# Decoder step: the sample stage begun in the last attention step's tail, w_out split early, and the spare rows' copies spread over attention steps

## What is computed

```python
q_g, k_g, v_g, r_g, log_a, q_a, k_a, v_a, gate_a, gate_b = combined_projection(h, w_in, gk_up, gk_bias)
# prompt: chunked gated linear attention and sliding-window attention
# sample: one recurrent step on a stored state, and attention over 128 cached keys
o_g, s_new = gla_run(q_g, k_g, v_g, log_a, gla_s0, ...)
o_a, k_new, v_new = swa_sample(q_a, k_a, v_a, win_k, win_v, rel_bias, sinks)
merged = sigmoid(gate_a) * gla_output(o_g, r_g) + sigmoid(gate_b) * o_a
h1 = layer_norm(ALPHA * h + merged @ w_out, ln1_g, ln1_b)
f  = hier_moe(h1, ...)          # 32 experts, each token goes to 2
h2 = layer_norm(ALPHA * h1 + f, ln2_g, ln2_b)
```

## Time and profile before

| | |
|---|---|
| median of 3 runs | 1911.17 us (1908.79 to 1911.86) |
| profiled execution, own time | 1909.03 us |
| its span, first to last instruction | 1906.9 us |
| busy: PE, PEld, DVE, ACT, POOL | 91%, 77%, 64%, 46%, 16% |
| mean granted TensorE clock | 0.944 of full speed |
| first step of stage B to end of the last | 331 to 965 us |
| sample stage | 965 to 1052 us |
| output stage | 1052 to about 1205 us |

### The profile page before, as it was taken

The page is one execution under the profiler, slowest core; times in us unless marked ns, Lnnn a source line. Parts: engine busy times, 40 slices in busy tenths (PEclk is TensorE's granted clock), DMA queues, the critical chain, the costliest instruction groups (busy, mean ns, idle before and its releaser), DMA issues. The chain is left out here.

```text
span 1906.9 us, 28797 instructions
## 1 busy us (share of the span) xinstructions
PE 1734.5 (91%) x9022; PEld 1463.8 (77%) x9022; DVE 1221.0 (64%) x1695; ACT 883.9 (46%) x1446; POOL 306.3 (16%) x386
## 2 busy tenths in 40 slices
PE   4899999899899999999978899379999999999955
PEld 4889999688788878878846788268888888888832
DVE  6411110577778767777753333868988988988917
ACT  4322221344344434444411122338778778788723
POOL 3200000122412232232210111010000010010025
PEclk9889999899999999999967899579999999999978
DMA  6379521434333333422359424379999999999854
GB/s 207 108 238 289 171 68 52 142 103 144 115 123 125 126 130 103 158 90 89 95 191 321 146 99 185 123 273 397 419 411 414 417 411 409 419 413 408 330 214 194
DMA packets 183312, 422.90 MB, mean 222 GB/s; under 512 B 24976, under 2 KB 123168, under 8 KB 158424
## 3 DMA queue, kind: packets, MB, share of 16 engines
q1 hardware_dynamic: 129776, 321.93, 45.8%
q0 software_dynamic: 20048, 69.06, 10.2%
q10 hardware_dynamic: 33408, 30.94, 4.6%
HBM read 354.83 MB, written 78.55 MB: 227 GB/s over the span
## 5 line engine op out<-in xcount | busy, mean ns | idle before, releaser
L1801 DVE TENSOR_TENSOR wm_lo<-raw,wm_hi 128x2048 fp32r<-128x2048 f32 x192 | 434.3, 2290 | 70.1 <-ACT wm_hi L1297 66.5
L1297 ACT CAST wm_hi<-raw 128x2048 fp32r<-128x2048 f32 x192 | 363.4, 1912 | 72.9 <-PE PS L1934 44.8
L1932 PE MATMUL PS<-w_hi,hT_hl 128*128 128x512 f32 (+1 forms) x584 | 232.9, 399 | 12.0 <-DMA hT_hl<-hl_dram 7.1
L1933 PE MATMUL PS<-w_lo,hT_hl 128*128 128x512 f32 (+1 forms) x584 | 227.0, 389 | 0.0
L1934 PE MATMUL PS<-w_hi,hT_hl 128*128 128x512 f32 (+1 forms) x584 | 226.6, 388 | 0.0
L1932 PE MATMUL PS<-wm_hi,xT_hi 128*128 128x512 f32 x512 | 203.7, 398 | 2.9 <-DVE xT_lo L1863 2.9
L1934 PE MATMUL PS<-wm_hi,xT_lo 128*128 128x512 f32 x512 | 200.8, 392 | 0.0
L1933 PE MATMUL PS<-wm_lo,xT_hi 128*128 128x512 f32 x512 | 200.3, 391 | 0.0
L1972 PE MATMUL PS<-xa_hi,wn 128*128 128x384 f32 x480 | 162.1, 338 | 0.2 <-ACT ev L1063 0.2
L1974 PE MATMUL PS<-xa_hi,wn 128*128 128x384 f32 x480 | 161.3, 336 | 0.0
L1973 PE MATMUL PS<-xa_lo,wn 128*128 128x384 f32 x480 | 161.2, 336 | 0.0
(11 more groups left out here) (340 smaller groups left out, 3403.2 us busy)
## 6 DMA issues: line engine op xcount, KB each, us to landing
raw<-in_w_gate SPq DMA_DIRECT2D x64, 1024.0 KB, 6.7
raw<-in_w_up SPq DMA_DIRECT2D x64, 1024.0 KB, 7.5
raw<-in_w_down SPq DMA_DIRECT2D x64, 1024.0 KB, 8.4
hT_hl<-hl_dram POOLq DMA_DIRECT2D x70, 512.0 KB, 5.2
braw<-in_w_in SPq DMA_DIRECT2D x16, 1024.0 KB, 6.2
obuf_dram<-yb ACTq DMA_DIRECT2D x32, 512.0 KB, 8.2
nd_dram<-ev ACTq DMA_DIRECT2D x72, 192.0 KB, 2.1
nd<-nd_dram SPq DMA_DIRECT2D x36, 384.0 KB, 3.4
```

The lines of the kernel that those rows point to most:

```text
L1297: act.copy(wm_hi[:, j], raw[:, j]).then_inc(m_hi[j // 4], 1)
L1801: dve.tensor_tensor(wm_lo[:, j], raw[:, j], BF(wm_hi[:, j]), ALU.subtract).then_inc(m_lo[j // 4], 1)
L1932: pe.matmul(out, x_hi, w_hi_, start=start, stop=False)
L1933: pe.matmul(out, x_hi, w_lo_, start=False, stop=False)
```

## The change

Three edits, which share the queues:

1. The sample stage starts without the common wait. PE, VectorE and GpSimd each wait only for what they touch; SP loads `gath` and `aqo` right after the last gates product. `S_MERGED` no longer holds back the output stage: `o_transposes(0, 0)` is put between the sample scores and the softmax on PE, `o_low(0, 0)` between the copy of `oT` and the merge on VectorE, ScalarE waits for `S_PV`, and L2150 writes to PSUM banks 6 and 7 so that banks 0 and 1 are free. The first two loads of `hh` come before the state stores.
2. Two of the four pieces of `w_out` are loaded and split in the last group's steps, where earlier groups split the next group's weights; the other two are loaded at its end and split in ScalarE's and VectorE's waits of the sample stage.
3. The two 4608 KB copies of the spare rows become 18 copies of 512 KB, two each in blocks 3, 4 and 5 of groups 0 to 2, issued by SP between `ka_load` and the next `nd_load`.

The diff, cut to its core (text in brackets stands for code that only moves or stays):

```diff
--- wait values
-    S_..., S_OTC, S_MERGED = (..., 21, 22)
+    S_..., S_OTC, S_OTREAD, S_MERGED = (..., 21, 22, 23)
...
--- SP (the sync engine's queue), attention steps
+        def spare_rows(k):
+            for a in range(2):
+                sp.dma_start(obuf_dram[(NE + a * NB + k) * P:(NE + a * NB + k + 1) * P, :], h_dram[k]).then_inc(s_out, 16)
...
                 ka_load(g, b, s, n0 + b)
+                if g < 3 and b in (3, 4, 5):
+                    spare_rows(3 * g + b - 3)
                 if g + 1 < G and b in (1, 7):
                     wide_load(g + 1, 0 if b == 1 else 2)
                 if g + 1 < G and b in (2, 8):
                     wide_load(g + 1, 1 if b == 2 else 3)
+                if g + 1 == G and b in (2, 3):
+                    wout_load(b - 2)
...
+        wout_load(3)
         sp.wait_ge(b_gg, upto(G * NB - 1))
+        stash_done(sp, G - 1)
+        (gath and aqo loads, moved up from behind stageB_done)
         state_load(0)
         state_load(1)
+        wout_load(2)
         stageB_done(sp)
-        (gath and aqo loads)
         state_load(2)
         state_load(3)
-        wout_load(0)
-        wout_load(1)
...
-        wout_load(2)
-        wout_load(3)
...
-        for a in range(2):
-            sp.dma_start(obuf_dram[(NE + a * NB) * P:(NE + (a + 1) * NB) * P, :],
-                         h_dram.rearrange("b p n -> (b p) n")).then_inc(s_out, 16)
         for k in range(2):
             mg_load(k, k)
+        sp.wait_ge(s_pe, S_SC)
+        h_load(0, 0)
+        h_load(1, 1)
         sp.wait_ge(s_dve, S_STATE[G - 1] + 1)
         (four stores of gla_state_sample, then the S_MERGED wait, as before)
-        h_load(0, 0)
-        h_load(1, 1)
         mg_load(2, 0)
-        sp.wait_ge(s_out, 16 * (G + 2))
+        sp.wait_ge(s_out, 16 * (G + 2 * NB))
--- GpSimd
-        stageB_done(pool)
+        pool.wait_ge(b_gg, upto(G * NB - 1))
--- ScalarE
+        def out_high(c):
+            act.wait_ge(w_raw[4 + c % 2], 16 * (c // 2 + 1))
+            act.wait_ge(b_gg, upto((G - 1) * NB - 1))
+            act.copy(wo_hi[:, 2 * c:2 * c + 2].rearrange("p k n -> p (k n)"), raw[:, 4 + c % 2]).then_inc(b_hi, 1)
...
                 for j in pieces:
-                    if j < 2:
+                    if j < 2 and g + 1 < G:
                         wide(g + 1, j)
+                    elif j < 2:
+                        out_high(j)
...
         stageB_done(act)
-        for c in range(4): (wait for the load and copy to wo_hi)
+        out_high(2)
+        out_high(3)
...
-        act.wait_ge(s_dve, S_MERGED)
+        act.wait_ge(s_pe, S_PV)
         (o_high(0, 0), o_high(1, 1), ... as before)
--- VectorE
+        def out_low(c):
+            dve.wait_ge(b_hi, upto(G * WIDE + c))
+            dve.tensor_tensor(wo_lo[:, 2 * c:2 * c + 2] ..., raw[:, 4 + c % 2], wo_hi[:, 2 * c:2 * c + 2] ..., ALU.subtract).then_inc(b_lo, 1)
...
                 for j in pieces:
-                    wide(g + 1, j)
+                    if g + 1 < G:
+                        wide(g + 1, j)
+                    elif j:
+                        out_low(2 - j)
...
-        stageB_done(dve)
+        dve.wait_ge(b_gg, upto(G * NB - 1))
+        stash_done(dve, G - 1)
         (in the loop over g of the state updates:)
-            dve.wait_ge(b_hi, upto(G * WIDE + g))
-            dve.tensor_tensor(wo_lo[:, 2 * g:2 * g + 2] ...).then_inc(b_lo, 1)
         mark(dve.reduce_sum(s8[:, 0], oQ, X), s_dve)
+        stageB_done(dve)
+        out_low(3)
+        out_low(2)
         dve.wait_ge(s_pe, S_SC)
...
         mark(last, s_dve)                 (oT copied)
+        o_low(0, 0)
         dve.wait_ge(act_s, 12)
...
-        link(dve.tensor_tensor(oQ, PS[0:NS, 0:2] ..., gath[:, :, 2], ALU.mult))
+        mark(dve.tensor_tensor(oQ, PS[0:NS, 6:8] ..., gath[:, :, 2], ALU.mult), s_dve)
+        dve.wait_ge(s_dve, S_OTREAD)
         mark(dve.tensor_tensor(oS, oS, oQ, ALU.add), s_dve)
-        dve.wait_ge(s_dve, S_MERGED)
         dve.wait_ge(o_small, 96)
-        o_low(0, 0)
         o_low(1, 1)
--- TensorE
-        stageB_done(pe)
-        pe.wait_ge(b_ko, upto(G - 1))
+        pe.wait_ge(b_stg, G)
+        for done in (b_bs, b_pc, b_pd, b_vrc, b_va, b_eg):
+            pe.wait_ge(done, upto(G * NB - 1))
...
         pe.wait_ge(s_win, 16 * 9)
+        pe.wait_ge(b_ko, upto(G - 1))
+        pe.wait_ge(b_oa, upto(G * NB - 1))
...
         last.then_inc(s_pe, 1)            (scores done)
+        pe.wait_ge(s_dve, S_SSQ - 1)
+        o_transposes(0, 0)
         pe.wait_ge(s_dve, S_ST)
...
-                last = pe.transpose(PS[0:NS, g // 2, c:c + HD], oT[:, h, g, :], ident[0:HD, 0:HD])
+                last = pe.transpose(PS[0:NS, 6 + g // 2, c:c + HD], oT[:, h, g, :], ident[0:HD, 0:HD])
...
-        pe.wait_ge(b_lo, upto(G * WIDE - 1 + 4))
-        pe.wait_ge(s_dve, S_MERGED)
-        pe.wait_ge(o_small, 96)
...
         def o_logits(b):
+            pe.wait_ge(s_dve, S_OTREAD)
+            pe.wait_ge(o_small, 96)
...
-        o_transposes(0, 0)
         o_transposes(1, 1)
+        pe.wait_ge(b_lo, upto(G * WIDE - 1 + 4))
         o_product(0, 0)
```

More of the change, by code:

```diff
@@ L670, in ka_load, with wout_load @@
                 sp.dma_start(ka[s][half * HD:(half + 1) * HD, :], nd_dram[g, b, 0:HD, 4 * P:5 * P]).then_inc(b_kd, 16)
+        wout = A["w_out"][0].rearrange("(k p) n -> p k n", p=P)
+        def wout_load(c):
+            if c >= 2:
+                sp.wait_ge(b_lo, upto(G * WIDE + 3 - c))
+            sp.dma_start(raw[:, 4 + c % 2].rearrange("p (k n) -> p k n", k=2),
+                         wout[:, 2 * c:2 * c + 2, :]).then_inc(w_raw[4 + c % 2], 16)
         sp.wait_ge(n_acc, len(units))
@@ L774, in h_load @@
             sp.dma_start(hh[s][:], h_dram[ds(blk(b), 1)].rearrange("o p n -> p (o n)")).then_inc(e_x[s], 16)
+        sp.wait_ge(s_pe, S_SC)
+        h_load(0, 0)
+        h_load(1, 1)
+        sp.wait_ge(s_dve, S_STATE[G - 1] + 1)
+        for g in range(G):
+            sp.dma_start(R["gla_state_sample"][0, :, g].rearrange("n k e -> k n e"), st[:, g]).then_inc(s_out, 16)
+        sp.wait_ge(s_dve, S_MERGED)
+        sp.dma_start(mg_dram[0, 0:NS, :], oS.rearrange("n g e -> n (g e)")).then_inc(s_new, 16)
+        sp.wait_ge(s_new, 48)
         def h1_store(b, s):
@@ L1185, in step @@
                 act.copy(va[s][:], PS[:, 5, 0:HD]).then_inc(b_va, 1)
-                if 2 in pieces:
+                if 2 in pieces and g + 1 < G:
                     wide(g + 1, 2)
@@ L1220, in _ @@
                 step(n0 + 2 + 2 * i, s0_, (n0 + 3) // 2 + i, False)
-            step(n0 + 5, s1_, (n0 + 6) // 2, False, (0,) if more else ())
-            step(n0 + 6, s0_, (n0 + 7) // 2, False, (1,) if more else ())
+            step(n0 + 5, s1_, (n0 + 6) // 2, False, (0,))
+            step(n0 + 6, s0_, (n0 + 7) // 2, False, (1,))
             step(n0 + 7, s1_, (n0 + 8) // 2, False)
-            step(n0 + 8, s0_, (n0 + 9) // 2, False, (2,) if more else ())
+            step(n0 + 8, s0_, (n0 + 9) // 2, False, (2,))
         stageB_done(act)
-        for c in range(4):
-            act.wait_ge(w_raw[4 + c % 2], 16 * (c // 2 + 1))
-            act.copy(wo_hi[:, 2 * c:2 * c + 2].rearrange("p k n -> p (k n)"), raw[:, 4 + c % 2]).then_inc(b_hi, 1)
+        out_high(2)
+        out_high(3)
         for a in range(8):
@@ L1607, in _ @@
                 step(n0 + 2 + 2 * i, s0_, (n0 + 3) // 2 + i, False, 0)
-            step(n0 + 5, s1_, (n0 + 6) // 2, False, 0, (0,) if more else ())
-            step(n0 + 6, s0_, (n0 + 7) // 2, False, 0, (1,) if more else ())
+            step(n0 + 5, s1_, (n0 + 6) // 2, False, 0, (0,))
+            step(n0 + 6, s0_, (n0 + 7) // 2, False, 0, (1,))
             step(n0 + 7, s1_, (n0 + 8) // 2, False, 0)
-            step(n0 + 8, s0_, (n0 + 9) // 2, False, 0, (2,) if more else ())
+            step(n0 + 8, s0_, (n0 + 9) // 2, False, 0, (2,))
             if g:
@@ L1685, in _, with o_low @@
         mark(last, s_dve)
+        def o_low(b, s):
+            dve.wait_ge(t_hi, upto(NB + b))
+            dve.tensor_tensor(mT_lo[s][:], PS[:, 0:2].rearrange("p a n -> p (a n)"), BF(mT_hi[s][:]), ALU.subtract).then_inc(t_lo, 1)
+        o_low(0, 0)
         dve.wait_ge(act_s, 12)
@@ L2134, in _, with o_transposes @@
         last.then_inc(s_pe, 1)
+        def o_transposes(b, s):
+            pe.wait_ge(h_in[s], 16 * (use(b, s) + 1))
+            pe.wait_ge(t_lo, upto(b - 1))
+            transposes(0, mg[s], KC).then_inc(t_T, 1)
+        pe.wait_ge(s_dve, S_SSQ - 1)
+        o_transposes(0, 0)
         pe.wait_ge(s_dve, S_ST)
```

35 lines of the change are left out of this document (10 added, 25 removed).

## The result

| | before | after |
|---|---|---|
| median of 7 runs each (lowest to highest), us | 1911.17 (1908.79 to 1914.93) | 1922.96 (1919.53 to 1930.26) |
| span of the profiled execution, us | 1906.9 | 1921.2 |
| mean granted clock | 0.944 | 0.944 |

The ratio is 1.0068, with a 95% interval of 1.0050 to 1.0085: the changed kernel is 0.7% slower, about 12 us. The forecast was 1906.0, a gain, and the time lies above the range.

The account below looks back on a forecast made before the run. It took PE, with small products and long pauses between stage B and the output stage, as the bound. Gains 2.2 - 1.6 + 7.5 - 0.7 = 7.4, less 2.7 and 0.6, left 4.1 us; forecast 1906.0, range 1900.5 to 1914.5.

Parts of the forecast that it names:

- 2.2: Start of the sample stage: gain in us up to `outer(1)`, limited by the state load rather than `outer(0)`'s 3.4.
- 1.6: Middle of the sample stage: us lost by putting `o_transposes(0, 0)` between the scores and the first softmax transpose.
- 7.5: End of the sample stage: us gained as value product to first output product shrinks from 11.94 to 4.4.
- the clock's 0.7: Output stage's first product: us lost to a longer low clock after thin work, bounds 0 and 1.8.
- What the spare rows' leaving gives back: nothing: Sample stage: 0 us gained by removing the spare copies, since nothing on the chain waits for a DMA after 984.75.
- 0.3 a step, the least of the waits seen: Stage B, blocks 3 to 5 of three groups: spare copies cost 2.7 us over nine steps, between 0 and 17.
- rival C: Stage B, blocks 4 to 6: copies hold up `hT` in all nine steps, deciding from 0.76 us each; 1914, chance 0.18.
- far case: Stage B: whole 2.8 us burst ahead of `hT`, 0.8 in hand; 2.0 us lost a step, nine 18, kernel 1920.
- signs of being wrong: Stage B waits above 0.8 us, waiting for `mg_load(2, 0)`, state loads no earlier, or over 4 us low clock in first product.
- `w_out` at 0.6: Stage B, last group: `w_out` loads in block 3 and at block 8's end cost 0.3 us each, range 0 to 3.9.
- B: Rival: stage B feels nothing from the new transfers and the 7.4 us gain is kept; 1903, chance 0.20.
- D: Rival: the sample stage gives only 0.8 us, state loads no earlier and clock rising late; 1909.5, chance 0.20.

Follow-up runs that it names:

- e8: The kernel before with only the spare rows' copies moved into stage B, issued behind the landing of the `hT` load: 1911.15 us, ratio 1.0001.
- e5: The kernel before with only the sample stage's early start; spare rows and all four `w_out` pieces stay in the sample stage: 1913.65 us, ratio 1.0016.
- e1: The kernel before with only the spare rows' 18 copies moved into the attention steps, as in the changed kernel: 1926.33 us, ratio 1.0076.
- e4: The changed kernel with each spare copy cut into rows of 4 KB instead of 32 KB, same bytes and place: 1925.44 us, ratio 1.0061 against before.
- e7: The changed kernel with one 512 KB copy a step ahead of `hT`, the other half one copy in the sample stage: 1906.12 us, ratio 0.9983 against before.
- e3: The changed kernel with the same 18 copies issued only after the next `hT` load has landed: 1905.74 us, ratio 0.9958 against before.
- e2: The changed kernel with the spare rows back in the sample stage as two large copies: 1910.02 us, ratio 0.9972 against before.
- e10: The kernel before with only the head groups' weight loads (`wide_load`) moved behind the `hT` load's landing: 1907.14 us, ratio 0.9975.
- e6: The changed kernel with spare copies, `wide_load`s and three `w_out` loads of stage B behind the `hT` load's landing: 1899.7 us, ratio 0.9949 against before.
- e11: The kernel before with the sample stage's early start, spare copies and `wide_load`s behind `hT`'s landing, `w_out` in the sample stage: 1898.0 us, ratio 0.9922.
- e9: The kernel before with the sample stage's early start and spare copies behind `hT`'s landing, `w_out` loaded and split as before: 1905.77 us, ratio 0.9977.

## Why the prediction was wrong

**Edit 1 was right, part by part.** With both traces laid on stage B's last scores, `outer(0)` starts at 976.9 in before's time (977.1 was said) and `outer(1)` at 985.3 (985.5), where PE started it at 987.5: 2.2 us for the **2.2**. `o_transposes(0, 0)` lies between scores and softmax, 1.90 long; from the scores' end to the value product's start it is 5.7 us instead of 4.4, 1.3 for the **1.6**. The last stretch is 4.39 for 4.4, the **7.5**. Only the clock's 0.7 did not come: full clock was there 1.3 us after the first product's start, before's 1.7. S gave 8.4 for 7.4. The `mg_load(2, 0)` with its 3 us to spare made no wait.

**"What the spare rows' leaving gives back: nothing" held for the kernel before (e8), not for the changed one.** The argument was that nothing on before's chain waits for a DMA after 984.75. But edit 1 itself pulls the first reader of `mg` 15 us forward, and e5 shows 8.5 us of wait there if `w_out` and spare rows are still ahead of it. That the 0 held in the sum was luck: edits 2 and 3 were in and had cleared the queue. The step counted a thing on the old chain that should have been counted on the new one.

**The term that failed is "0.3 a step, the least of the waits seen", nine steps, 2.7.** It measured 14.1, 1.6 a step (14.7 in e1, 15.8 in e4). The mechanism was in the prediction: rival C has the copies holding up `hT`, the decision point of 0.76 us, and a far case of 2.0 a step and 1920. Its place was one block late. Rival C and the signs of being wrong name blocks 4, 5 and 6; the copies hold up the `hT` of the block that issues them, 3 to 5, and the waits stood in blocks 3 and 5 and not in 4 or 6. The runs came close to the far case, by two amounts that no term had:

- The wait itself was 8.6 us over six steps, 1.4 in each of the six. The prediction had all that is needed: 2.8 us of copies, 0.8 us in hand, a `wide_load` of the same size that cost up to 1.93. Passing time less what is in hand gives 2.0 a step, an upper figure for the 1.4. The reason to choose the least was that contiguous pieces pass more quickly than pieces of 1 KB. e4 refutes it for 4 against 32 KB: what counts is how many bytes are ahead (e7: half of them, hardly a wait), and whether they are ahead at all (e3: behind, no wait). Three steps in nine were spared, because the stall before them turned the order round; no one counted on that.
- The low clock behind a stall was counted in the sample stage alone. In stage B it came behind three of the six waits, about 5.1 us for 8.6 of waiting; e1 has the same (8.9 and three dips), e4 8.7 and four.

**`w_out` at 0.6 was 2.5**, the same mistake on two loads. The other **5.0** of stage B have no term either; they lie in steps that waited as before but had more of the low clock. No run ties them to the copies: the same steps cost 0.7 more than before in e1, 1.8 in e4, which has all three edits, and 1.5 less in e3. How much of them is this one execution stays open.

**Rivals.** B fell (e1). D fell: the stretch gave its gain. C was right in mechanism, one block off in place, with 14 against its 10.4 and 18; its chance of 0.18 was too low, since before's own rows showed the wait behind five of six loads of this size, and three such steps in a row in each group.

Shown by runs: that edit 3 makes the loss (e1, e2), that it is the order of copies and `hT` (e3), by their bytes (e4, e7), and that before paid the same behind its own loads (e10, e6). The split of the 14.1 into waits and clock is read from traces, and three of them agree (after, e1, e4). Open: the 5.0, and what sets the clock in the sample stage.

## What to carry to other kernels

A bulk transfer without a deadline should be issued behind the load that the bound engine needs next, by a wait on that load's landing; the same 18 copies cost some 14 us ahead of it and nothing behind it, and the rule was worth 5 to 6 us more on loads that had always been there. For a transfer that shares the DMA engines with a just-in-time load, take its whole passing time less what the load has in hand as the price to fear (2.0 here, for 1.4 measured), and not the smallest wait seen; then add the half-speed time that can follow a stall of PE. And when an edit pulls work forward, list what that work reads and what stands ahead of those loads in the new order: a transfer that delayed nobody before can be the bound now.

## What the runs showed of the hardware that was not expected

A wait of 1.2 to 1.7 us of PE, in a stretch that is otherwise full, was followed in three of six cases by 3.4 us at a granted clock of 0.5, which doubles its price; in the other three it was not; e1 had it three times in six too, e4 four times. Which it will be could not be told from the rows.

In the stretch of the `outer`s and the read-outs the granted clock can fall with PE 100% busy. Two windows of 19 us in that stretch, of e3 and of e6:

```profile
998.00:1017.00 19.00, 19.00 (x90) 10.70 (x88) 7.29 (x17) 0.11 (x1) 0.00 (x0) 1.00 0.31 80
```

```profile
995.00:1014.00 19.00, 19.00 (x66) 8.46 (x65) 4.75 (x12) 0.00 (x0) 0.00 (x0) 0.73 0.15 54
```

e3 does 90 matmuls there at a clock of 1.00, e6 66 at 0.73, from the same lines; the four read-outs and the last two `outer`s took 23.4 us in the one (from 992.85) and 27.9 in the other (from 985.72). It happened in the profiled execution of e2, e5, e6, e10 and e11, and not in that of before, after or the other six. S was 6.8 us longer in e2 than in after, 5.9 in e11 than in e9, 3.3 in e6 than in e3, and no longer in e10 than in before, where the fall was a single one of 3.4 us. So in these executions it takes back most of edit 1 in e2 and e11. Whether it belongs to the kernel or to the execution can't be told, since each kernel has one trace; what decides it stays open, and no run was made for it.
